# Latent attention and mLSTM on one core: the last sigmoid ahead of gate rows and weights, key rounding on VectorE, score products ahead of the last division

## The chip, the core and the metric

The kernel runs on one core of a Trainium2 chip. The metric is the device time of one execution in microseconds. The core has a matmul engine (TensorE, PE in the profile, with its weight loads as PEld), a vector engine (VectorE, DVE), an activation engine (ScalarE, ACT), GpSimd (POOL) and SyncE (SP), which issues the transfers. Each engine works through its own queue in order; semaphores order the engines among each other.

## The reference, cut to what matters

One step of a trunk of two layers over 640 tokens (128 context, 512 latent), model width 1024. Every layer is SwiGLU, mixer, SwiGLU. The mixer of layer 0 holds the change; it adds a latent attention with 8 heads to an mLSTM with 4 heads run in both directions over chunks of 128 tokens:

```python
q_a, kv_a, k_rope, mq, mk, mv, mo, mg = jnp.split(h @ w_in, EVEN_SPLIT_IDX, axis=-1)
ckv = rmsnorm(kv_a, g_kva)
q = (rmsnorm(q_a, g_qa) @ w_qb)                       # 8 heads of 64 + 32 (rope)
kv = keys_ckv @ w_kvb                                 # 8 heads of 64 (keys) + 64 (values)
k = concatenate([kv[..., :64], keys_kr (same for all heads)])
attn = softmax(q k^T / sqrt(96)) v
...                                                   # mLSTM, per head and direction, per chunk
a = einsum('bhtd,bhsd->bhts', qc, kc) * exp(dmat - mt)
hm = (h_forward + h_backward), rms-normalised, * g_mout
m_out = sigmoid(mo) * hm
y = concatenate([attn, m_out], -1) @ w_out
```

## The kernel before

Activations lie feature-major (features on partitions, 640 tokens on the free axis). Nearly all large products keep float32 precision with three passes: a weight tile is rounded by ACT to `w_hi` (L411), DVE subtracts to get `w_lo` (L417), and PE multiplies hi*hi, hi*lo and lo*hi. The same split is made for the operands of the attention scores: `k_top`/`k_rest` and `q_top`/`q_rest`. PSUM has 8 banks of 512 float32 columns; the code numbers them.

The mixer of layer 0 runs once, between some 540 and 900 us. It has three stages, in this order on every engine.

Input projection (`pe_even_in`, `act_even_in`, `dve_even_in`). Eight rounds of two weight chunks. The last two groups (`pe_token_major`) put token-major results into PSUM: `mv` into banks 0 to 4, then `mo` into banks 5, 6, 0, 1, 2, one bank per chunk of 128 tokens. ACT empties them with `fill(which, c)`: a copy into `v_m`, a sigmoid into `mo` (L804), each adding one to `l_vfill`. Between these ACT and DVE work on the small "rows" of the gates; `act_rows_columns` (L1233 to L1239) reads bank 7, takes exponentials into `floors` and raises `r_columns`. In the last round (b == 7) ACT's order is: round a weight chunk, four sigmoids, round the next weight chunk (the first one of the output projection), `act_rows_columns`, the fifth sigmoid, and then an activation table load (L1867). Before it starts the attention, PE waits for all ten `l_vfill` and for `r_columns`.

Latent attention (`pe_mla`, `act_mla`, `dve_mla`). The order of the work is a list, `MLA_PLAN`, built once by `mla_plan()`; each engine walks the same list and does its part of each entry. "swap", "turned", "keys", "queries" and "values" build q, k and v from the latent tensors (L552, L526, L535 on PE; copies on ACT, rope on DVE). For each head: "stage", "stage2" and "stage3" are ACT copies that round the raw query into `q_top` (L643, L644), the raw key into `k_top` (L646) and the rope rest into `q_rest` (L649); "rest" is DVE's two subtractions (L700, L702); nine "unit" entries are score products whose maxima DVE reduces (L573, L708) to a per-query shift; "shift" spreads the maxima (L577, L579), ACT writes them into `q_top` (L652). Seven "scores" entries (L593 to L595) make the scores of 128 keys by all queries, ACT takes the exponential (L658) and "attend" multiplies with the values (L603, L610). The units of head h+1 are interleaved with the scores x = 2, 3, 4 of head h; they wait for `e_hi`, which ACT raises at the end of `k_top`. ACT's entries for head h+1 stand behind scores 0 ("stage"), 1 ("stage2") and 3 ("stage3") of head h. "divisor" (ACT: Ln, Exp, L666, L668) and "divide" (DVE, L723, raising `e_scaled`) normalise a head, "high"/"low" (L671, L727) split the result of a pair of heads into `hx_hi`/`hx_lo`; "low" raises `o_done`.

mLSTM (`pe_mlstm`, `act_mlstm`, `dve_mlstm`). PE first waits for all four `o_done`, then makes the raw score products of keys and queries in six groups `KQ_GROUPS` (L1326; group (two, e) holds one or two chunks and one row half) and transposes the keys (L1316, banks 5 to 7); ACT scales the products into `kq` (L1400). DVE, after its own `o_done` wait, multiplies `mo` by the gain (L1444, five instructions) and then scales the transposed keys into `ktok` (L1447, L1449). With `kq` and `ktok` in place the chunk loop over `ML_PLAN` begins (L1305 on PE).

After it follow the output projection of the mixer and the other sub-layers, whose first transfers and roundings are triggered by counts (`w_used`), not by time.

## Time and profile before

| | us |
|---|---|
| median of 3 runs | 2782.93 |
| lowest and highest | 2778.52, 2784.07 |
| profiled execution, its own time | 2783.91 |
| its span in the trace | 2782.0 |
| PE busy, share of the span | 95% |
| DVE busy, share of the span | 54% |
| ACT busy, share of the span | 38% |
| mean granted clock of PE | 0.974 |

1.9 us of the profiled execution lie outside the span. The page counts PE as busy 95% of the time, but its slices between 600 and 900 us are the ones below nine tenths; the time of a stage is read there from the timeline of each engine, with the idle time before an instruction in brackets and the instruction that ended it. PEclk is the share of full clock granted to PE: 1.00 is 2.4 GHz and 0.50 is 1.2 GHz.

### The profile page before, as it was taken

How to read it: one execution, taken by the hardware profiler on the slowest of the kernel's cores; microseconds unless marked ns; L12 is line 12 of the kernel's file. 1: busy time of each engine (PE TensorE's matmuls, PEld its weight loads, DVE VectorE, ACT ScalarE, POOL GpSimd, SP SyncE). 2: the span in 40 equal slices, each digit the busy share in tenths (PEclk: the TensorE clock that was granted, in tenths of full speed). 3: DMA queues.
4: the chain of work that ended last, by engine and by line, in shares of the span. 5: the costliest groups of instructions: out<-in, count | busy, mean ns of one | idle time of the engine just before them, and what ended most of it. 6: DMA issues, size and time to landing. Idle time of an engine off the chain costs nothing.

```text
span 2782.0 us, 41236 instructions
## 1 busy us (share of the span) xinstructions
PE 2637.4 (95%) x16851; PEld 2498.3 (90%) x16871; DVE 1490.8 (54%) x2403; ACT 1053.1 (38%) x1599; POOL 3.7 (0%) x5
## 2 busy tenths in 40 slices
PE   6999999998887899999999999999989989999998
PEld 6999999885456889999999999999978889999998
DVE  6888434633446377753367775346565436322334
ACT  4333334444553453223345222334433345222333
POOL 0000000000000000000000000000000000000000
PEclk7999999999988999999999999999989999999999
DMA  6666244320000246533446553344210024322344
GB/s 239 208 203 207 77 134 147 133 71 24 1 0 24 61 148 203 187 114 103 146 140 196 191 187 98 110 148 140 89 45 1 1 61 119 102 74 75 107 149 139
DMA packets 87770, 320.18 MB, mean 115 GB/s; under 512 B 12486, under 2 KB 16598, under 8 KB 87126
## 3 DMA queue, kind: packets, MB, share of 16 engines
q1 hardware_dynamic: 87638, 318.37, 35.4%
q8 instruction: 88, 1.44, 0.2%
q14 instruction: 44, 0.36, 0.0%
HBM read 312.44 MB, written 3.23 MB: 113 GB/s over the span
## 4 chain that ended last, share of the span: by engine, by line
PE 85%; DVE 8%; ACT 4%; issue 2%; DMA 2%; SPq 1%; another core or an unknown queue 0%; DVEq 0%; ACTq 0%
PE ps L2179 42%; PE ps L2208 29%; PE ps L990 2%; PE ps L746 2%; DVE w_lo L417 1%; PE ps L603 1%; ACT w_hi L411 1%; DMA w_raw<-in_ffn_gu 1%; PE ps L552 1%; PE ps L2242 1%; PE ps L976 1%; DVE xsq L1967 1%; PE ps L979 1%; PE ps L978 1%; DVE hx_lo L1976 1%
## 5 line engine op out<-in xcount | busy, mean ns | idle before, releaser
L417 DVE TENSOR_TENSOR w_lo<-w_raw,w_hi 128x1024 fp32r<-128x1024 f32 (+1 forms) x384 | 521.0, 1358 | 901.5 <-ACT w_hi L411 898.7
L411 ACT CAST w_hi<-w_raw 128x1024 fp32r<-128x1024 f32 (+1 forms) x384 | 443.7, 1156 | 1212.5 <-PE ps L2179 715.1
L2179 PE MATMUL ps<-hx_hi,w_hi 128*128 128x320 f32 x2688 | 614.3, 309 | 11.8 <-DVE hx_lo L1526 5.7
L2179 PE MATMUL ps<-hx_lo,w_hi 128*128 128x320 f32 x2688 | 613.3, 309 | 0.0
L2179 PE MATMUL ps<-hx_hi,w_lo 128*128 128x320 f32 x2688 | 613.1, 309 | 0.0
L2179 PEld LDWEIGHTS ps<-hx_hi,w_hi 128*128 128x128 f32 x2688 | 451.4, 188 | 13.1 <-issue 7.6
L2179 PEld LDWEIGHTS ps<-hx_hi,w_lo 128*128 128x128 f32 x2688 | 451.8, 188 | 0.0
L2179 PEld LDWEIGHTS ps<-hx_lo,w_hi 128*128 128x128 f32 x2688 | 451.7, 188 | 0.0
L2208 PE MATMUL ps<-hh_hi,w_hi 128*128 128x320 f32 x1408 | 435.4, 309 | 3.0 <-DVE hh_lo L2071 3.0
L2208 PE MATMUL ps<-hh_hi,w_lo 128*128 128x320 f32 x1408 | 433.2, 308 | 0.0
L2208 PE MATMUL ps<-hh_lo,w_hi 128*128 128x320 f32 x1408 | 433.2, 308 | 0.0
L2208 PEld LDWEIGHTS ps<-hh_hi,w_hi 128*128 128x128 f32 x1408 | 263.9, 187 | 4.7 <-issue 3.9
L2208 PEld LDWEIGHTS ps<-hh_lo,w_hi 128*128 128x128 f32 x1408 | 263.9, 187 | 0.6
L2208 PEld LDWEIGHTS ps<-hh_hi,w_lo 128*128 128x128 f32 x1408 | 263.9, 187 | 0.0
L2208 PE MATMUL ps<-hx_hi,w_hi 128*128 128x320 f32 x672 | 222.0, 330 | 29.5 <-DVE hx_lo L1976 21.1
L2208 PE MATMUL ps<-hx_lo,w_hi 128*128 128x320 f32 x672 | 213.8, 318 | 0.0
L2208 PE MATMUL ps<-hx_hi,w_lo 128*128 128x320 f32 x672 | 213.8, 318 | 0.0
L2208 PEld LDWEIGHTS ps<-hx_hi,w_hi 128*128 128x128 f32 x672 | 131.0, 195 | 45.5 <-issue 21.3
L2208 PEld LDWEIGHTS ps<-hx_lo,w_hi 128*128 128x128 f32 x672 | 132.3, 197 | 0.5
L2208 PEld LDWEIGHTS ps<-hx_hi,w_lo 128*128 128x128 f32 x672 | 132.1, 197 | 0.0
L1904 DVE SCALAR_TENSOR_TENSOR ada_junk<-ring_a,cond_b 128x1024 f32<-128x1024 f32 x96 | 117.1, 1220 | 3.7 <-DVE ring_a L1904 0.5
L1904 DVE SCALAR_TENSOR_TENSOR ring_a<-ring_a,cond_b 128x1024 f32<-128x1024 f32 x96 | 117.1, 1220 | 0.0
(298 smaller groups left out, 2634.3 us busy)
## 6 DMA issues: line engine op xcount, KB each, us to landing
w_raw<-in_ffn_gu SPq DMA_DIRECT2D x212, 512.0 KB, 3.6
w_raw<-in_ffn_dn SPq DMA_DIRECT2D x128, 704.0 KB, 4.1
ring_a<-in_ada_w SPq DMA_DIRECT2D x96, 512.0 KB, 4.6
ada_top<-in_ada_w SPq DMA_DIRECT2D x32, 512.0 KB, 4.6
w_raw<-in_even_in SPq DMA_DIRECT2D x16, 512.0 KB, 3.6
w_raw<-in_odd_in SPq DMA_DIRECT2D x12, 512.0 KB, 4.7
first_a<-in_ada_w SPq DMA_DIRECT2D x8, 512.0 KB, 12.2
w_raw<-in_even_out SPq DMA_DIRECT2D x8, 512.0 KB, 3.7
```

What stands on the lines that cost most here:

```text
L411: nc.scalar.copy(w_hi[:, slot, 0:tiles * P], w_raw[:, slot, 0:tiles * P]).then_inc(hi_done, 1)
L417: nc.vector.tensor_tensor(w_lo[:, slot, 0:tiles * P], w_raw[:, slot, 0:tiles * P], w_hi[:, slot, 0:tiles * P], ALU.subtract).then_inc(lo_d ...
L552: ins = nc.tensor.matmul(ps[:, bank + n, 0:b - a], w_qb[:, k, tile * P:(tile + 1) * P], pa[:, k, a:b], start=(k == 0), stop=(k == 1))
L603: nc.tensor.matmul(ps[:, 6 + two, :], value_ones(x, h), prob_e[:, b % 3, :], start=(x == 0), stop=(x == 5)).then_inc(e_pv, 1)
L746: last = nc.tensor.matmul(ps[:, tok_bank(which, c), :], a[:, 2 * i + k, c * P:(c + 1) * P], w[:, q, cols], start=i == 0 and k == 0 and a i ...
L976: nc.tensor.matmul(out, ones_r[:], diag_o[:, g["g"] % 4].rearrange("p i q -> p (i q)"), start=True, stop=False)
L978: nc.tensor.matmul(by_head, k_hi[:, h, kcol:kcol + P], queries, start=False, stop=False)
L979: ins = nc.tensor.matmul(by_head, k_lo[:, h, kcol:kcol + P], queries, start=False, stop=side is None)
L990: ins = nc.tensor.matmul(ps[:, 6 + g["g"] % 2, i * (HEAD + 1):(i + 1) * (HEAD + 1)], prob_o[:, b % 4, i * P:(i + 1) * P], v_aug[:, g["bloc ...
L1904: ins = nc.vector.scalar_tensor_tensor(out=product, in0=tile, scalar=1.0, in1=cond_b[:, ci, :], op0=ALU.mult, op1=ALU.mult, accum_out=mods ...
L2179: last = nc.tensor.matmul(ps[:, out_bank + h, 0:TH], w, a[:, k, h * TH:(h + 1) * TH], start=(start and w is wh and a is hi), stop=(stop an ...
L2208: last = nc.tensor.matmul(ps[:, bank, 0:TH], w, a[:, k0 + t, half(h)], start=first and t == 0 and w is wh and a is hi, stop=last_chunk and ...
```

## The change

It does four things.

1. In the last round of the input projection ACT takes the fifth sigmoid first, then `act_rows_columns`, then the rounding of the next weight chunk. PE's wait for all sigmoids and for `r_columns` ahead of the attention is split: "swap" (now in banks 3 and 4) starts with the five `v_m` copies done, "turned" (banks 6 and 7) waits for two sigmoids and `r_columns`, "queries" (banks 0 and 1) for all sigmoids.
2. "stage2", the rounding of the key into `k_top`, is done by DVE with a semaphore of its own, `e_khi`; `e_hi` is raised at the end of ACT's query copies. "stage2" and "stage" stand together behind scores 0.
3. In the mLSTM, PE no longer waits for `o_done`. Groups (0,0), (0,1), (1,1), (2,0) of the score products follow the last attend at once; group (1,0), in bank 1, waits for the eighth `e_scaled`, and the transposes and group (2,1) follow it.
4. ACT scales the products into `kq` ahead of its wait for `o_done` and for the stored outputs.

```diff
--- before.py
+++ after.py
@@ -70,8 +70,8 @@
             if before:
                 plan.append(("attend",) + before)
             before = (h, x)
-            if h + 1 < MLA_HEADS and x in (0, 1, 3):
-                plan.append(({0: "stage", 1: "stage2", 3: "stage3"}[x], h + 1, 0))
+            if h + 1 < MLA_HEADS and x in (0, 3):
+                plan += [("stage2", h + 1, 0), ("stage", h + 1, 0)] if x == 0 else [("stage3", h + 1, 0)]
             if h and x in (2, 3):
                 plan.append(({2: "divisor", 3: "divide"}[x], h - 1, 0))
             if h + 1 < MLA_HEADS and x == (2 if h % 2 == 0 else 5):
@@ -332,7 +332,7 @@
         e_built, e_raw, e_vfill = sem("e_built"), sem("e_raw"), sem("e_vfill")
         e_rope_t, e_rope, e_rope_hi, e_rope_lo = sem("e_rope_t"), sem("e_rope"), sem("e_rope_hi"), sem("e_rope_lo")
         kr_ready, rows_clear, gates_moved = sem("kr_ready"), sem("rows_clear"), sem("gates_moved")
-        e_hi, e_rows, e_lo = sem("e_hi"), sem("e_rows"), sem("e_lo")
+        e_hi, e_khi, e_rows, e_lo = sem("e_hi"), sem("e_khi"), sem("e_rows"), sem("e_lo")
         e_unit, e_max, e_diag, e_shift, e_neg = sem("e_unit"), sem("e_max"), sem("e_diag"), sem("e_shift"), sem("e_neg")
         e_st, e_p, e_pv, e_inv, e_scaled = sem("e_st"), sem("e_p"), sem("e_pv"), sem("e_inv"), sem("e_scaled")
         odd_out, odd_turned, odd_rope = sem("odd_out"), [sem("odd_turned0"), sem("odd_turned1")], sem("odd_rope")
@@ -488,7 +488,7 @@
 
             if kind == "values":
                 return (2, 3, 4, 5, 0, 1, 6)[i]
-            return {("keys", 0): 4, ("turned", 0): 6}.get((kind, i), 0)
+            return {("swap", 0): 3, ("keys", 0): 4, ("turned", 0): 6}.get((kind, i), 0)
 
         def value_pairs(x):
 
@@ -541,11 +541,15 @@
                         pe.wait_ge(e_raw, 2 * i + 1)
                     else:
                         pe.wait_ge(e_rope_t, 1)
+                        pe.wait_ge(l_vfill, 2 * CHUNKS)
                 elif i:
                     if kind == "swap":
                         pe.wait_ge(e_raw, 5)
                     else:
                         pe.wait_ge(e_rope_t, 2)
+                elif kind == "turned":
+                    pe.wait_ge(l_vfill, CHUNKS + 2)
+                    pe.wait_ge(r_columns, 1)
                 tile = {"queries": i, "turned": 4 + 2 * i, "swap": 5 + 2 * i}[kind]
                 for n, (a, b) in enumerate(((CTX, T), (0, CTX))):
                     for k in range(2):
@@ -563,6 +567,7 @@
                     u, bank = 9 * h + x, 2 + (9 * h + x) % 2
                     if x == 0:
                         pe.wait_ge(e_hi, h + 1)
+                        pe.wait_ge(e_khi, h + 1)
                         if h == 0:
                             pe.wait_ge(e_vfill, 2)
                         else:
@@ -641,9 +646,7 @@
                     if h >= 2:
                         act.wait_ge(e_st, 7 * (h - 1))
                     nc.scalar.copy(q_top[0:64, two, :], raw_q[0:64, h % 2, :])
-                    nc.scalar.copy(q_top[64:96, two, :], rope_hi[stack_rows(h), :].bitcast(F32))
-                elif kind == "stage2":
-                    nc.scalar.copy(k_top[0:64, two, :], raw_k[0:64, h % 2, :]).then_inc(e_hi, 1)
+                    nc.scalar.copy(q_top[64:96, two, :], rope_hi[stack_rows(h), :].bitcast(F32)).then_inc(e_hi, 1)
                 elif kind == "stage3":
                     act.wait_ge(e_rope_lo, h // 4 + 1)
                     nc.scalar.copy(q_rest[64:96, two, :], rope_lo[stack_rows(h), :].bitcast(F32)).then_inc(e_rows, 1)
@@ -680,7 +683,12 @@
 
             for kind, h, x in MLA_PLAN:
                 two = h % 2 if h is not None else 0
-                if kind == "swap":
+                if kind == "stage2":
+                    dve.wait_ge(e_raw, 2 * (h // 2) + 1)
+                    if h >= 2:
+                        dve.wait_ge(e_st, 7 * (h - 1))
+                    nc.vector.tensor_copy(k_top[0:64, two, :], raw_k[0:64, h % 2, :]).then_inc(e_khi, 1)
+                elif kind == "swap":
                     dve.wait_ge(e_built, MLA_BUILT[kind, x])
                     nc.vector.tensor_tensor(rope_t[:], ps[:, build_bank(kind, x), :], rope_e[:, 1, :],
                                             ALU.mult).then_inc(e_rope_t, 1)
@@ -696,6 +704,7 @@
                     nc.vector.tensor_tensor(rope_lo[:, LAT:T], flat(bank, LAT, T), rope_hi[:, LAT:T].bitcast(F32),
                                             ALU.subtract).then_inc(e_rope_lo, 1)
                 elif kind == "rest":
+                    dve.wait_ge(e_khi, h + 1)
                     dve.wait_ge(e_hi, h + 1)
                     nc.vector.tensor_tensor(k_rest[0:64, two, :], raw_k[0:64, h % 2, :], k_top[0:64, two, :].bitcast(F32),
                                             ALU.subtract)
@@ -779,8 +788,7 @@
             pe_token_major(pe, chunk, 1, 2)
             pe_rows_columns(pe)
             pe_token_major(pe, chunk, 1, 3)
-            pe.wait_ge(l_vfill, 2 * CHUNKS)
-            pe.wait_ge(r_columns, 1)
+            pe.wait_ge(l_vfill, CHUNKS)
             pe.wait_ge(mix_loaded, 16 * 7)
             pe.wait_ge(lora_ready, 3)
             pe.wait_ge(attn_const, 6)
@@ -823,13 +831,14 @@
                     link(act, act_chain, nc.scalar.activation(halves(lora[:, 4, :]), bank_pair(3), ACT.Ln,
                                                               bias=eps_col[:, 0:1], scale=1.0 / P))
                     nc.scalar.activation(lora[:, 3:5, :], lora[:, 3:5, :], ACT.Exp, scale=-0.5).then_inc(lora_rstd, 1)
+                if b == 7:
+                    fill(1, CHUNKS - 1)
+                    act_rows_columns(act)
                 split_hi(act, 2 * b + chunk + 3, 1, 8)
                 if b < 4:
                     evacuate(2 * b + 1)
-                elif b == 7:
-                    act_rows_columns(act)
-                if b in (5, 7):
-                    fill(b // 7, CHUNKS - 1)
+                elif b == 5:
+                    fill(0, CHUNKS - 1)
                 if b == 3:
                     act.wait_ge(in_loaded, CONSTS)
                     zero, one = (ident[96:P, c:c + 1].unsqueeze(1) for c in (0, 96))
@@ -1188,7 +1197,7 @@
 
             return (j, 0) if u == 0 else (u - 1, j + 1)
 
-        KQ_GROUPS = [(two, e) for two in range(3) for e in range(2)]
+        KQ_GROUPS = [(0, 0), (0, 1), (1, 1), (2, 0), (1, 0), (2, 1)]
 
         def kq_chunks(two):
 
@@ -1308,7 +1317,6 @@
                     ins = nc.tensor.matmul(ps[:, d, :], ident_b[:], causal_b[:, d].rearrange("p i q -> p (i q)"),
                                            start=False, stop=True)
                 return ins
-            pe.wait_ge(o_done, MLA_OUT)
             def turned_keys():
                 for c in range(CHUNKS):
                     for j in range(2):
@@ -1316,6 +1324,8 @@
                         ins = nc.tensor.transpose(ps[:, 5 + c // 2, a:a + P], mqk[:, 2 + j, c * P:(c + 1) * P], ident[:])
                 ins.then_inc(l_turned, 1)
             for two, e in KQ_GROUPS:
+                if (two, e) == (1, 0):
+                    pe.wait_ge(e_scaled, MLA_HEADS)
                 if (two, e) == (2, 1):
                     turned_keys()
                     pe.wait_ge(l_kq, len(KQ_GROUPS) - 1)
@@ -1392,14 +1402,14 @@
 
         def act_mlstm(act):
 
-            act.wait_ge(o_done, MLA_OUT)
-            act.wait_ge(out_stored, 48)
             for i, (two, e) in enumerate(KQ_GROUPS):
                 act.wait_ge(l_turned, i + 1 + (i == len(KQ_GROUPS) - 1))
                 cs, a = kq_chunks(two), kq_start(two, e)
                 nc.scalar.activation(kq[:, e::2, cs[0]:cs[-1] + 1, :].rearrange("p h c q -> p c h q"),
                                      ps[:, kq_bank(two, e), a:a + 256 * len(cs)].rearrange("p (c h q) -> p c h q", h=2, q=P),
                                      ACT.Copy, scale=M_DK ** -0.5).then_inc(l_kq, 1)
+            act.wait_ge(o_done, MLA_OUT)
+            act.wait_ge(out_stored, 48)
             for kind, u in ML_PLAN:
                 two = u % 2
                 if kind == "decays":
```

## Rows read from the trace of the kernel before

**Rows 1.** Timeline of ACT, 654 to 660: start, duration, instruction [idle before, releaser]

```profile
654.37 1.04 ACT L411 CAST w_hi<-w_raw 128x1024 fp32r<-128x1024 f32 x1 [1.15 <-PE ps L746]
...
657.00 0.21 ACT L1239 ACTIVATE floors<-ps 128x16 f32<-128x16 f32 x1
...
658.52 0.60 ACT L804 ACTIVATE mo<-ps 128x512 f32<-128x512 f32 x1
```

**Rows 2.** Timeline of PE, start of the attention, same columns

```profile
659.17 7.51 PE L552 MATMUL ps<-pa,w_qb 128*128 128x512 f32 x16 [5.19 <-ACT mo L804]
...
668.02 2.33 PE L552 MATMUL ps<-pa,w_qb 128*128 128x512 f32 x8
```

**Rows 3.** Windows: length, busy PE, PEld, DVE, ACT, POOL, PEclk, DMA, GB/s

```profile
659.00:660.00 1.00, 0.83 (x1) 0.50 (x2) 0.00 (x0) 0.98 (x2) 0.00 (x0) 0.50 0.00 0
...
788.00:789.50 1.50, 1.50 (x6) 1.11 (x5) 0.69 (x1) 0.20 (x1) 0.00 (x0) 0.50 0.00 0
...
849.50:851.00 1.50, 1.50 (x8) 1.50 (x8) 1.47 (x4) 0.78 (x2) 0.00 (x0) 0.50 0.98 391
```

**Rows 4.** Timelines of DVE, ACT and PE ahead of the first maxima

```profile
655.45 1.23 DVE L417 TENSOR_TENSOR w_lo<-w_raw,w_hi 128x1024 fp32r<-128x1024 f32 x1 [6.51 <-ACT w_hi L411]
...
677.24 2.75 DVE L708 TENSOR_REDUCE e_mx<-ps 128x1 f32<-128x512 f32 x5
...
668.17 0.62 ACT L629 CAST rope_hi<-rope_raw 128x512 fp32r<-128x512 f32 x1 [7.76 <-DVE rope_raw L691]
...
674.53 0.94 ACT L646 CAST k_top<-raw_k 64x896 fp32r<-64x896 f32 x1
...
675.80 1.03 PE L573 MATMUL ps<-k_top,q_top 96*128 96x512 f32 x2
```

**Rows 5.** Waits, 683 to 826: who waited for whom, us in total, times, longest

```profile
PE ps L573 <- ACT k_top L646: 11.4, 7, 1.9
```

**Rows 6.** Timelines: ACT and PE at head 2's first unit, DVE at head 5's

```profile
707.61 0.72 ACT L644 CAST q_top<-rope_hi 32x640 fp32r<-32x640 f32 x1
...
708.97 0.94 ACT L646 CAST k_top<-raw_k 64x896 fp32r<-64x896 f32 x1
...
709.96 0.50 PE L573 MATMUL ps<-k_top,q_top 96*128 96x512 f32 x1 [1.92 <-ACT k_top L646]
...
767.57 0.69 DVE L708 TENSOR_REDUCE e_mx<-ps 128x1 f32<-128x512 f32 x1 [5.32 <-PE ps L573]
```

**Rows 7.** Groups of instructions, 683 to 826: busy us, mean ns, idle before

```profile
L700 DVE TENSOR_TENSOR k_rest<-raw_k,k_top 64x896 fp32r<-64x896 f32 x7 | 7.5, 1075 | 0.0
```

**Rows 8.** Timeline of PE: the first units of heads 1 and 4

```profile
689.97 0.50 PE L573 MATMUL ps<-k_top,q_top 96*128 96x512 f32 x1 [0.72 <-ACT k_top L646]
...
752.41 0.50 PE L573 MATMUL ps<-k_top,q_top 96*128 96x512 f32 x1 [1.29 <-ACT k_top L646]
```

**Rows 9.** Timeline of PE: shift of head 4, first unit and shift of head 6

```profile
760.57 0.50 PE L577 MATMUL ps<-diag_e,ones_r 128*128 128x512 f32 x1
...
787.55 0.50 PE L573 MATMUL ps<-k_top,q_top 96*128 96x512 f32 x1 [1.79 <-ACT k_top L646]
...
797.34 0.51 PE L577 MATMUL ps<-diag_e,ones_r 128*128 128x512 f32 x1
```

**Rows 10.** Timelines of DVE, ACT and PE, from the last division to the chunk loop

```profile
827.37 0.90 DVE L723 TENSOR_TENSOR o_raw<-ps,e_rec 64x512 f32<-64x512 f32 x2 [5.44 <-ACT e_rec L668]
...
829.92 3.10 DVE L1444 TENSOR_TENSOR mo<-mo,w_raw 128x512 f32<-128x512 f32 x5
...
836.80 1.23 DVE L1447 TENSOR_SCALAR ktok<-ps 128x1024 f32<-128x1024 f32 x1 [3.78 <-PE ps L1316]
...
828.31 0.72 ACT L671 CAST hx_hi<-o_raw 128x640 fp32r<-128x640 f32 x1 [0.97 <-DVE o_raw L723]
...
829.94 5.30 PE L1326 MATMUL ps<-mqk 64*128 64x128 f32 x36 [4.16 <-DVE hx_lo L727]
...
838.50 1.26 PE L1305 MATMUL ps<-gstack,pick 128*128 128x128 f32 x8 [1.10 <-DVE ktok L1449]
```

## The prediction

> **What bounds the kernel now.** I read the page first, then the timelines of PE, ACT and DVE from 636 to 862 us, the list of waits between 683 and 826, and the granted clock in short windows. The page's part 1 has PE busy nearly throughout, so away from the mixer of layer 0 a reordering of the other engines has nothing to win, and the change touches nothing there. In this mixer PE stands idle in three places, and the timeline names the releaser of each. Ahead of the attention it is idle 5.19 us, and the fifth sigmoid ends it [rows 2]. In the attention it waits for the rounding of `k_top` seven times, 11.4 us in total [rows 5]. After the last head it waits 4.16 us for `hx_lo` [rows 10]. That is 20.7 us. A second cost goes with it: behind such a gap the granted clock can be at its lower level, 1.2 GHz (0.50), for some microseconds [rows 3]. Everything behind the mixer waits on counts of finished work, so what is gained here arrives at the end one to one.
>
> **Part 1: the end of the input projection.** PE's last product ends at 653.98 (659.17 less 5.19) [rows 2]. ACT reacts at 654.37 with the weight rounding of 1.04, then come the gate rows, then the fifth sigmoid until 659.12 [rows 1]. With the change PE begins "swap" at once: its banks 3 and 4 held `v_m`, emptied long before. "Swap" and "turned" are 16 records and took 7.51 us from a low clock [rows 2, 3]; 8 such records at the full clock take about 2.2 (2.33 with the drain of the last) [rows 2]. With no gap the clock stays up, so "swap" ends at about 656.1.
> "Turned" must wait for `r_columns`. This was raised at 657.21, 1.80 us after the rounding had ended at 655.41 [rows 1]. Now a sigmoid of 0.60 stands in the place of that rounding: 654.37 + 0.60 + 1.80 = 656.8. "Turned" runs from 656.85 to about 659.0 instead of ending at 666.6: 7.6 us earlier. A table load (back to the sigmoid's set) falls away too, off this path.
> The weight rounding moves behind the gate rows, to 656.7 to 657.8, and DVE's `w_lo` of 1.23 [rows 4] follows it, to 659.0. It stands in DVE's queue ahead of the rope of "swap", finished by PE at 656.1. Who waits for that: "queries" on PE, which stands behind "keys" and is needed near 660.5, while the rope is ready at 659.7, so no cost; and the rope of "turned", which comes out about 0.45 late. ACT's chain therefore starts with `rope_hi` at 661.05 instead of 668.17 [rows 4], 7.1 earlier. The weight chunk itself, and SP's next load into its slot, are used only after the mLSTM, 200 us later; no cost.
> In the first head ACT's `k_top` ended at 675.47 and DVE's first maximum started at 677.24, 1.77 after it, because DVE's "rest" lies between [rows 4]. With `k_top` on DVE (in its idle time before 667), "rest" waits for ACT's `q_top` alone, which ended when `k_top` began, at 674.51. So "rest" starts at 674.51 - 7.1 = 667.4 and the first maximum at 669.2. PE's first unit comes at 675.80 [rows 4] less 7.6, 668.2, and is done by then. DVE's maxima set the time here, and they are 677.24 - 669.2 = 8.0 us earlier. **Part 1 with the first head: 8.0 us.**
>
> **Part 2: heads 1 to 7.** At head 2 ACT does `q_top` until 708.33, an exponential of 0.60, then `k_top` until 709.91, and PE starts the first unit at 709.96 after 1.92 idle [rows 6]. With `k_top` off ACT, the unit is released at 708.38, 1.58 earlier. DVE is idle there: the shortest gap before a head's first maximum is 5.32 [rows 6], so its copy is hidden, and I cost it at nothing. No row of before has a DVE copy of this form. Its time lies between that of ACT, 0.94 [rows 6], or somewhat less, and that of DVE's subtraction over as many elements, 1.08 [rows 7]; I take 1.0, and if the cover were gone the seven would cost 7 us. The copy waits for the scores of head h-1; behind that wait DVE's queue holds only this head's maxima, which need the copy anyway.
> PE's idle is 0.72 and 1.29 before heads 1 and 4 [rows 8], which leaves 11.4 - 2.0 = 9.4 for the other five [rows 5], 1.88 each. The gains are 0.72 + 1.29 + 5 x 1.57 = 9.9. What is late next is ACT's `q_top`, by 0.3. The second wait per first unit may cost 0.04 each (an estimate: 0.05 lies between a releaser's end and PE's start [rows 6]), 0.3 in all. **9.6 us.**
> The clock: from first unit to shift head 4 took 760.57 - 752.41 = 8.16, head 6 with the same work 797.34 - 787.55 = 9.79 [rows 8, 9], with 0.50 granted at its start [rows 3]. A fall costs 1.6 there. Heads 5 and 7 have falls too; DVE's "rest" covers part of them, and I take 0.7 each, between 0 and 1.6. All three follow a gap of nearly 2 us that shrinks to 0.3: **3.0 us**, bounds 0 and 4.8.
> [...]
>
> **Part 3: into the mLSTM.** PE ends the attention at 825.78 (829.94 less 4.16). Four groups of score products follow at once, and group (1,0) finds its division done at 828.27 [rows 10]. Even at the pace of before, products and transposes take what they took from 829.94 to 836.80, 6.86, and end at 832.7. ACT starts on `kq` after `hx_hi`, at 829.03 [rows 10], and needs at most 0.60 each (the sigmoid of the same shape [rows 1]): five are done by 832.1, in time for group (2,1). DVE's work on `mo` ends at 829.92 + 3.10 = 833.02. DVE was then idle 3.78 us for the transposes; now `ktok` starts at 833.05 instead of 836.80 and the chunk loop at 834.75 instead of 838.50 [rows 10]: **3.75 us**. What is late next is the work on `mo`, that is `o_done` itself. ACT's last `kq` stays hidden behind `ktok`. The moved wait for stored outputs costs nothing: they are issued at the end of the input projection.
> The Trainium skill (TensorE: Matmul & The Clock Gate, Part 4) says that transposes do not count as PE activity. By it the clock could fall in the wait for `ktok`, behind the ten transposes; the first 8 spread records, 1.26 [rows 10], would then take up to twice that, and this part would be 2.5. No row here shows it.
>
> **The sum.** 8.0 + 9.6 + 3.0 + 3.75 = 24.4 us. The profiled execution took 2783.9 (span 2782.0 and 1.9 around it), 1.0 above the median. 2783.9 - 24.4 = 2759.5, or 2758.5 against the median. I say 2759.
>
> **The rivals.**
> First, the clock gives nothing. Low spells come elsewhere when the gaps are gone: the 3.0 in the heads stay, and "swap" and "turned" (or what follows them) lose again what the full clock gave them, 7.51 - 4.4 = 3.1. Gain 18.3, time 2765.6. For it: the mLSTM, with its short bursts, has such a spell while PE is busy [rows 3]. Against: the spells at 659 and 788 both follow idle time.
> Second, the heads do not move, because what is left of ACT's chain or DVE's maxima hold them: 8.0 + 3.75 = 11.8, time 2772. Against: PE's wait names `k_top` in seven heads of seven [rows 5].
> Third, slower: DVE's in-order queue. Were the wait for the old scores reached late, or the copy held behind "rest" and maxima, each first unit would come later than ACT delivered it. Seven heads at d each outweigh parts 1 and 3 from d = 11.8 / 7 = 1.7 us on, that is if the copy of head 2 ends after 711.6. With d = 3 the time is 2783.9 - 11.8 + 21 = 2793. Against: 5.32 us of idle DVE at the tightest place [rows 6].
> Fourth, part 1 does not do what it says: "turned" waits on `r_columns` long enough for the clock to fall, and only 3 of the 8.0 us come. Time 2764.5.
>
> **How the numbers follow.** Forecast 0.62 (its own range 2753 to 2764); first and fourth rival 0.26; second 0.08; third 0.02; the rest, near no change, 0.02. A measurement tells 0.2% from no change, 5.6 us, so under 2777.4 is faster: faster 0.95, same 0.03, slower 0.02. The low end, 2752, takes in the lowest run of before (4.4 below the median) and one more low spell gone. The high end takes in the first and fourth rival and half of the way to the second: 2769.
>
> **What would show it.** Right: the first L552 near 654 with no sigmoid as releaser, `rope_hi` near 661, PEclk 1.00 there; at most 0.4 us idle before each head's first unit, ended by `q_top`; head 6 at 8.2 us from unit to shift; the first L1326 with no idle before it, and `ktok` directly behind the work on `mo`. Wrong: `k_top` from DVE later than `q_top`, 1 us of idle or more before the units with another name in the brackets, or a PEclk of 0.50 where it was 1.00.

## The result and the profile after

| | before | after |
|---|---|---|
| median, us | 2781.38 (4 runs) | 2757.95 (4 runs) |
| lowest and highest | 2778.52, 2784.07 | 2757.47, 2759.45 |
| profiled execution, its own time | 2783.91 | 2759.45 |
| its span | 2782.0 | 2757.6 |

The ratio of the times is 0.9923, with a 95% interval from 0.9909 to 0.9938: 21.4 us, and 17 to 25 by the interval. The two profiled executions are 24.46 us apart; the forecast for them was 24.4. That of before lies 2.5 us above its median and that of after 1.5 above its own. The page of after:

```profile
span 2757.6 us, 41258 instructions
...
PE 2629.5 (95%) x16851; PEld 2495.4 (90%) x16871; DVE 1495.8 (54%) x2411; ACT 1043.6 (38%) x1590; POOL 3.7 (0%) x5
```

The shares of the page are what they were. The change is seen only in timelines, stage by stage. First the end of the input projection, in the timelines of ACT, PE and DVE of after (start, duration, instruction, and in brackets the idle time before it and the releaser):

```profile
654.11 0.60 ACT L812 ACTIVATE mo<-ps 128x512 f32<-128x512 f32 x1 [0.80 <-PE ps L755]
...
654.80 1.28 ACT L1245 ACT_TABLE_LOAD   x1
...
656.35 1.07 ACT L411 CAST w_hi<-w_raw 128x1024 fp32r<-128x1024 f32 x1
...
660.63 0.62 ACT L634 CAST rope_hi<-rope_raw 128x512 fp32r<-128x512 f32 x1 [1.92 <-DVE rope_raw L699]
...
653.91 2.32 PE L556 MATMUL ps<-pa,w_qb 128*128 128x512 f32 x8
656.63 2.40 PE L556 MATMUL ps<-pa,w_qb 128*128 128x512 f32 x8 [0.40 <-ACT floors L1248]
...
668.14 1.03 PE L578 MATMUL ps<-k_top,q_top 96*128 96x512 f32 x2
...
674.99 0.80 PE L582 MATMUL ps<-diag_e,ones_r 128*128 128x512 f32 x1 [1.57 <-DVE diag_e L723]
...
663.15 0.62 DVE L690 CAST k_top<-raw_k 64x896 fp32r<-64x896 f32 x1 [0.82 <-ACT raw_k L631]
...
668.98 2.77 DVE L717 TENSOR_REDUCE e_mx<-ps 128x1 f32<-128x512 f32 x5
```

Of the idle time before the first L556, 5.19 us in [rows 2], nothing is left for "swap", and 0.40 for "turned". `rope_hi` comes 7.54 us earlier than in [rows 4], the first maximum 8.26 us, and the shift of head 0 (the spread of its maxima) 8.06 us (683.05 before).

Then the heads. Timeline of PE in after, the first units of heads 2 and 6, the queries ahead of head 4 and the shift of head 6:

```profile
699.96 0.50 PE L578 MATMUL ps<-k_top,q_top 96*128 96x512 f32 x1 [0.35 <-ACT q_top L649]
...
731.87 2.43 PE L556 MATMUL ps<-pa,w_qb 128*128 128x512 f32 x8 [1.71 <-DVE rope_lo L704]
...
769.10 0.50 PE L578 MATMUL ps<-k_top,q_top 96*128 96x512 f32 x1 [0.21 <-ACT q_top L649]
...
777.25 0.50 PE L582 MATMUL ps<-diag_e,ones_r 128*128 128x512 f32 x1
```

The list of waits of after, in the attention (us in total, times, longest):

```profile
PE ps L578 <- ACT q_top L649: 1.5, 5, 0.4
```

Windows of after (length, busy PE, PEld, DVE, ACT, POOL, then PEclk, DMA share and GB/s):

```profile
672.00:676.00 4.00, 2.03 (x5) 1.08 (x4) 3.02 (x7) 0.07 (x1) 0.00 (x0) 0.50 0.00 0
676.00:680.00 4.00, 3.33 (x7) 2.45 (x8) 0.00 (x0) 2.25 (x4) 0.00 (x0) 0.50 0.00 0
...
690.00:790.00 100.00, 90.94 (x327) 51.89 (x325) 55.71 (x104) 60.36 (x101) 0.00 (x0) 1.00 0.00 1
812.00:816.00 4.00, 2.74 (x9) 2.17 (x10) 0.87 (x3) 1.40 (x6) 0.00 (x0) 0.50 0.30 70
```

The row of [rows 5], 11.4 us in seven waits for `k_top`, has become 1.5 us in five waits for `q_top`. The windows show the other half of it: 1.00 granted over a hundred microseconds of heads, where before had 0.50 at 788 [rows 3]. But they also show a low spell (a stretch at 0.50) at 672 to 682.5, before and behind head 0's shift, and one at 812, at the start of the mLSTM.

Last, the way into the mLSTM, in the timelines of ACT, DVE and PE of after:

```profile
807.07 2.32 ACT L1408 ACTIVATE kq<-ps 128x512 f32<-128x512 f32 x5
...
808.06 3.10 DVE L1454 TENSOR_TENSOR mo<-mo,w_raw 128x512 f32<-128x512 f32 x5
811.18 1.23 DVE L1457 TENSOR_SCALAR ktok<-ps 128x1024 f32<-128x1024 f32 x1
...
803.85 3.77 PE L1336 MATMUL ps<-mqk 64*128 64x128 f32 x36
807.55 1.31 PE L1324 MATMUL ps<-ident,mqk 128*128 128x128 f32 x10
809.45 0.71 PE L1336 MATMUL ps<-mqk 64*128 64x128 f32 x4 [0.59 <-ACT kq L1408]
812.89 2.29 PE L1314 MATMUL ps<-gstack,pick 128*128 128x128 f32 x8 [2.73 <-DVE ktok L1459]
...
892.02 0.56 PE L2189 MATMUL ps<-hx_hi,w_hi 128*128 128x320 f32 x2 [1.59 <-DVE w_lo L417]
```

`ktok` follows the work on `mo` with no idle, where DVE had waited 3.78 us [rows 10]. The chunk loop starts 25.61 us earlier than before (812.89 against 838.50), and its first eight products take 2.29 us where they took 1.26 [rows 10]. The row at 892.02 belongs to the output projection behind the mLSTM. The timeline of PE in before has it at 916.47:

```profile
916.47 0.56 PE L2179 MATMUL ps<-hx_hi,w_hi 128*128 128x320 f32 x2 [1.60 <-DVE w_lo L417]
```

The lead there is 24.45, and it stays so to the end: from that row on both kernels take the same time, 1865.6 and 1865.5 us of the span.

### The profile page after: what moved, and what is told of

Same layout as the page of the kernel before. It is cut to its first block, busy times and chain, and to the rows that moved or that the text cites. A ratio compares the mean times of both kernels' runs of the same rounds, so it can differ in the third digit from the quotient of the medians.

```text
span 2757.6 us, 41258 instructions
## 1 busy us (share of the span) xinstructions
PE 2629.5 (95%) x16851; PEld 2495.4 (90%) x16871; DVE 1495.8 (54%) x2411; ACT 1043.6 (38%) x1590; POOL 3.7 (0%) x5
## 4 chain that ended last, share of the span: by engine, by line
PE 84%; DVE 7%; ACT 4%; DMA 2%; issue 2%; SPq 1%; another core or an unknown queue 0%; DVEq 0%; ACTq 0%
PE ps L2189 42%; PE ps L2218 29%; PE ps L999 2%; PE ps L755 2%; DVE w_lo L417 1%; PE ps L608 1%; ACT w_hi L411 1%; DMA w_raw<-in_ffn_gu 1%; PE ps L2252 1%; PE ps L985 1%; PE ps L556 1%; PE ps L988 1%; PE ps L987 1%; PE ps L578 0%; DMA w_raw<-in_odd_in 0%
```

## The experiments

The theory: the three parts act at their own places and add up, and a part of the gain in the heads is the clock's. Its rivals: the clock gives nothing; the copy on DVE is near its limit; the parts cover each other. Each ratio is against runs of the kernel before on the same chip. Timelines and windows are of one execution of each kernel.

### Each part alone

**e1, part 1 alone.**

```diff
-            pe.wait_ge(l_vfill, 2 * CHUNKS)
-            pe.wait_ge(r_columns, 1)
+            pe.wait_ge(l_vfill, CHUNKS)
...
+                if b == 7:
+                    fill(1, CHUNKS - 1)
+                    act_rows_columns(act)
                 split_hi(act, 2 * b + chunk + 3, 1, 8)
```

> The first part alone (fifth sigmoid first, swap in banks 3 and 4, split waits); heads and mLSTM as before. Theory (gains by idle time removed, clock kept up through swap and turned, one to one to the end): first maximum of head 0 near 669.0 instead of 677.2, and 8.0 us at the end, time about 2776 against a profiled before of 2783.9. Rival (the clock gives nothing): swap and turned fast, but a low spell later; gain 5. The unknown between them is which heads have a low spell once all is shifted by 8 us: each costs 0.7 to 1.7.

Measured: median 2772.33, ratio 0.9971 (0.9962 to 0.9981), that is 8.1 us, 5 to 11 by the interval. "Turned" in the timeline of PE:

```profile
656.30 1.10 PE L556 MATMUL ps<-pa,w_qb 128*128 128x512 f32 x2 [0.40 <-ACT floors L1243]
```

The heads' wait in the list of waits (us in total, times, longest):

```profile
PE ps L577 <- ACT k_top L650: 10.6, 6, 1.9
```

The start is that of after, and the heads wait for `k_top` as in before (the first of the seven waits lies ahead of the stretch of this list, 683 to 826). Head 0's shift comes at 675.51, 7.54 us earlier than before: in head 0 the rounding of the key is still ACT's here.

**e2, part 2 alone.**

```diff
+                if kind == "stage2":
+                    dve.wait_ge(e_raw, 2 * (h // 2) + 1)
+                    if h >= 2:
+                        dve.wait_ge(e_st, 7 * (h - 1))
+                    nc.vector.tensor_copy(k_top[0:64, two, :], raw_k[0:64, h % 2, :]).then_inc(e_khi, 1)
```

> The second part alone (key rounding on DVE, e_hi at the end of the query copies). Theory: idle before the first units shrinks from 11.4 to about 1.5 us, worth 9.6, and the low spells inside heads 5, 6 and 7 go with the gaps, worth 3.0 and perhaps the one at 743 (1.7) as well; head 6 takes 8.2 us from first unit to shift. Gain 12.6 to 14.3, time 2769.6 to 2771.3. Rival (clock gives nothing): gain 9.6, time 2774.3. Rival (heads held elsewhere): under 3.

Measured: median 2767.63, ratio 0.9958 (0.9943 to 0.9972), 11.7 us, 8 to 16 by the interval. Timeline of PE, first unit and shift of head 6:

```profile
775.01 0.50 PE L574 MATMUL ps<-k_top,q_top 96*128 96x512 f32 x1 [0.22 <-ACT q_top L645]
...
783.16 0.50 PE L578 MATMUL ps<-diag_e,ones_r 128*128 128x512 f32 x1
```

A window over the heads, with PEclk third from the end:

```profile
690.00:810.00 120.00, 109.68 (x393) 62.95 (x392) 62.35 (x117) 70.28 (x118) 0.00 (x0) 1.00 0.00 1
```

Head 6 takes 8.15 us from unit to shift, against 9.79 in [rows 9], and no window of the heads is below full clock. The spells in them go with part 2 alone. The median gained less than the 12.6 to 14.3 us expected, and its interval takes in that range as well as the rival's 9.6.

**e3, part 3 alone.**

```diff
-        KQ_GROUPS = [(two, e) for two in range(3) for e in range(2)]
+        KQ_GROUPS = [(0, 0), (0, 1), (1, 1), (2, 0), (1, 0), (2, 1)]
...
-            pe.wait_ge(o_done, MLA_OUT)
...
+                if (two, e) == (1, 0):
+                    pe.wait_ge(e_scaled, MLA_HEADS)
```

> The third part alone (score products of the mLSTM behind the last attend, key scaling copies ahead of the wait for o_done). Theory: ktok starts directly behind the work on mo, 3.75 us earlier relative to the end of the attention, of which about 1 is lost when the clock falls in the wait for ktok, so that the spread products run at 1.2 GHz; gain 2.8 to 3.8, time 2780 to 2781. If the three parts add up, e1, e2 and e3 give 8.0 + 13.5 + 3 = 24.5; a sum off by over 2 would mean that a part's gain hangs on another's.

Measured: median 2777.41 of 10 runs against 2779.3 of 20, ratio 0.9997 (0.9987 to 1.0007): 0.8 us, and 3.6 at most by the interval. Timeline of PE:

```profile
822.98 3.77 PE L1327 MATMUL ps<-mqk 64*128 64x128 f32 x36
...
832.02 1.64 PE L1305 MATMUL ps<-gstack,pick 128*128 128x128 f32 x5 [2.73 <-DVE ktok L1450]
```

From the end of the attention to the chunk loop it takes 9.0 us (822.98 to 832.02), before took 12.72 (825.78 to 838.50), after 9.0. So the 3.7 us are gained at their place. From there to the first product of the output projection it takes 59.60 us, and 58.42 in the profiled execution of before: 1.2 go back. What is left, some 2.5, a timing of this kernel hardly tells from nothing.

That 2.5 hangs on the one execution of before. Kernels e1 and e2 above and e5 below have its mLSTM too. From the end of the attention to the output projection before took 71.14 us, and e1, e2 and e5 took 72.06, 72.32 and 72.00; after took 68.62, e3 68.64 and e11, which is after once more, 68.51. By these part 3 is worth 2.5 to 3.8 us.

The three ratios fall short of 1 by 0.0029, 0.0042 and 0.0003, together 0.0074, and the whole change by 0.0077. The parts add up as far as such intervals can tell, which is some 6 us (a rough estimate from the four intervals); that none covers another is seen better in the timelines, each part acting at its own place.

### The cover of the copy

**e4, the copy three times.** After, with two superfluous copies ahead of each one that counts:

```diff
+                    for _ in range(2):
+                        link(dve, dve_chain, nc.vector.tensor_copy(k_top[0:64, two, :], raw_k[0:64, h % 2, :]))
```

> The changed kernel, with DVE's rounding of the key done three times in a row (each waits for the one before) for every head. One copy took 0.62 us, so each head's k_top is ready about 1.4 us later. Theory (the copy is hidden, q_top on ACT releases the unit): no change, idle before the first units of heads 2, 3 and 7 stays 0.35 and is still ended by q_top; time within 0.5 us of the changed kernel (2759.5 profiled). Rival (DVE's queue sets the heads): 7 x 1.4 = 10 us slower, 2769.

Measured: median 2758.27, ratio 0.992 (0.9904 to 0.9937), as after. Timelines of DVE and PE at head 2:

```profile
694.26 1.27 DVE L691 CAST k_top<-raw_k 64x896 fp32r<-64x896 f32 x2 [3.00 <-PE ps L600]
695.57 0.62 DVE L692 CAST k_top<-raw_k 64x896 fp32r<-64x896 f32 x1
...
698.84 0.50 PE L578 MATMUL ps<-k_top,q_top 96*128 96x512 f32 x1 [0.35 <-ACT q_top L649]
```

The third copy ends at 696.2, the unit starts 2.6 us later, and it is still `q_top` that releases it, after the same 0.35 us. The slower rival, DVE's in-order queue, was far from deciding there, and the median shows nothing of it either.

### What the clock gives

**e5, the gaps of before filled.** Before, with five superfluous score products (into the bank that the next unit overwrites) ahead of the first units of heads 2 to 7, where PE waits for `k_top` anyway:

```diff
+                    if x == 0 and h:
+                        pe.wait_ge(e_neg, h)
+                        pe.wait_ge(e_max, u - 1)
+                        for n in range(5 if h > 1 else 0):
+                            nc.tensor.matmul(ps[:, bank, 0:512], q_top[0:MLA_QK, 1 - two, 0:P],
+                                             k_top[0:MLA_QK, 1 - two, 0:512], start=True, stop=True)
```

> The kernel before, with five superfluous score products (96x128 by 512, 0.235 us each at the full clock, some 1.2 us together) ahead of PE's wait for the first unit of heads 2 to 7, written into the bank that the unit then overwrites. The first unit is still released by k_top, so no wait ends earlier. Theory (the gap costs twice: once as idle time and once by the lower clock behind it): the low spells behind the first units of heads 5, 6 and 7 and the one at 743 do not appear, the time falls by 2 to 5 us below the kernel before and scatters less than its 2772.6 to 2783.9. Rival (the clock gives nothing, the gain of the second part is idle time alone): low spells at the same or other places, time unchanged.

Measured: median 2779.21, ratio 0.9992 (0.9983 to 1.0002). Windows over the heads, first of this kernel:

```profile
694.00:821.00 127.00, 115.44 (x417) 68.06 (x418) 57.24 (x109) 75.65 (x123) 0.00 (x0) 1.00 0.00 0
```

then of the kernel before:

```profile
694.00:825.00 131.00, 114.32 (x387) 65.59 (x387) 57.47 (x109) 75.06 (x123) 0.00 (x0) 0.95 0.00 0
```

With the gaps filled the clock stays at 1.00 and the attention takes 162.4 us, where the profiled execution of before took 166.6. But e3, whose attention is that of before, took 163.8: how many of the gaps are followed by a fall differs from one execution to the next. The traces of all kernels tell it best between the shift of head 1 and that of head 7 (us, from the timelines of PE):

| | head 1's shift | head 7's shift | between | low spells |
|---|---|---|---|---|
| before | 702.82 | 813.80 | 110.98 | 4 |
| e1, same heads | 695.27 | 805.77 | 110.50 | 4 |
| e3, same heads | 702.22 | 811.09 | 108.87 | 3 |
| e5, gaps filled | 702.58 | 809.43 | 106.85 | 0 |
| after | 694.39 | 791.96 | 97.57 | 0 |

The other eight kernels with part 2 (e2, e4 and e6 to e11) took 97.51 to 97.58, and none has a spell there. So the spells do follow from the gaps: they cost 4.1, 3.7 and 2.0 us in the three executions, and the gaps themselves 9.3.

The medians of before and e5 are only 1.6 us apart, under the 2 to 5 expected, and the interval takes in no change. A part may be that e5's low spell in heads 0 and 1 is longer: it ends at 692.6, that of before at 689.0, and from the shift of head 0 to that of head 1 e5 took 1.24 us more. The scatter did change: ten runs within 2.9 us, while those of before range over 10.7 (13 runs on that chip), and those of e1 and e3, which keep the gaps, over 11.9 and 9.6. The gaps are not its only cause: e7 and e10, which have none in these heads, range over 11.2 and 9.3.

**e9, "swap" waits too.** After, with the waits of before ahead of "swap" (ACT's new order stays):

```diff
-            pe.wait_ge(l_vfill, CHUNKS)
+            pe.wait_ge(l_vfill, 2 * CHUNKS)
+            pe.wait_ge(r_columns, 1)
```

> The changed kernel with PE's waits for all sigmoids and r_columns back ahead of swap; ACT's new order and the banks stay. PE is then idle from 654.0 to 656.6. Theory (the fourth rival is a matter of the gap's length; before, the clock fell 4.6 us after PE had stopped): the gap of 2.6 us is too short for a fall, swap and turned stay at the full clock and end at 661.1 instead of 658.9, 2.2 us slower at the first maximum and at the end, 2760. Rival (any idle wait costs the clock): turned ends near 664, 5 us slower, 2763.

Measured: median 2760.25, ratio 0.9926 (0.9908 to 0.9944). After itself, run beside it as **e11** with no edit, gave 2757.7, ratio 0.9919 (0.9901 to 0.9937).

> The changed kernel as it is, to have it on the same chip beside e9 and e10. Expected 2758, and 0.992 of the kernel before; heads without low spells again, low spells at 671 to 683 and from 812 on.

Timeline of PE in e9:

```profile
655.70 6.25 PE L556 MATMUL ps<-pa,w_qb 128*128 128x512 f32 x16 [2.52 <-issue]
```

and a window of it:

```profile
656.00:660.00 4.00, 4.00 (x9) 1.90 (x8) 1.33 (x2) 1.81 (x2) 0.00 (x0) 0.57 0.02 4
```

(`issue` stands where the profile shows no releaser; by the code the wait is for the fifth sigmoid and `r_columns`.) A gap of 2.52 us was enough for a fall here: the sixteen products took 6.25 us, against 2.32 and 2.40 in after. That I had not expected of so short a gap. Head 0's shift comes at 677.73, in e11 at 674.46: 3.3 us for a gap of 2.5 us, which replaces one of 0.4. The medians are 2.5 apart, with intervals that overlap. In part 1, then, some 60 to 70% is ACT's order, and the rest that "swap" waits for nothing.

### The start of the mLSTM

**e6, 18 superfluous transposes** and **e7, 11 superfluous products** in the wait for `ktok`, into a free bank, both on after:

```diff
+            for n in range(18):
+                nc.tensor.transpose(ps[:, 3, P * (n % 4):P * (n % 4) + P], mqk[:, 2 + n % 2, 0:P], ident[:])
```

```diff
+            for n in range(11):
+                nc.tensor.matmul(ps[:, 3, P * (n % 4):P * (n % 4) + P], mqk[:, 2 + n % 2, 0:P], mqk[:, n % 2, 0:P],
+                                 start=True, stop=True)
```

> The changed kernel, with 18 superfluous transposes of 128x128 (0.13 us each, 2.4 us together) in PE's 2.73 us gap between the last score products of the mLSTM and the spread products. Theory A (transposes do not count as PE activity): the clock still falls near 812 and the first 8 spread products still take 2.3 us; time as the changed kernel, 2758. Theory B (only idle time lets it fall): they take 1.26 and the fall comes later or not; up to 1 us faster.

> The same gap filled with 11 superfluous products of 128x128 (22 records of 0.11 us, 2.4 us together). Both theories: the clock stays up at 812, the first 8 spread products take 1.26 us and the chunk loop gains about 1 us there, of which the later low spells in the loop may take some back. If e6 and e7 look alike, what fills the gap does not matter; if only e7 keeps the clock, transposes do not count.

Measured: medians 2754.9 and 2756.73, ratios 0.9904 (0.9888 to 0.9921) and 0.9904 (0.988 to 0.9928). Timeline of PE in e6:

```profile
809.58 2.19 PE L1340 MATMUL ps<-ident,mqk 128*128 128x128 f32 x18
812.38 0.63 PE L1314 MATMUL ps<-gstack,pick 128*128 128x128 f32 x4 [0.61 <-DVE ktok L1461]
```

windows of e6:

```profile
811.00:815.00 4.00, 2.25 (x17) 1.72 (x15) 1.54 (x3) 1.59 (x7) 0.11 (x1) 0.99 0.29 66
815.00:819.00 4.00, 1.57 (x7) 1.57 (x8) 1.83 (x4) 0.59 (x3) 0.00 (x0) 0.50 0.00 0
```

and one of e7:

```profile
811.00:815.00 4.00, 3.58 (x29) 3.10 (x28) 2.00 (x3) 0.78 (x4) 0.91 (x1) 1.00 0.24 66
```

In both the clock stays up over the first products of the chunk loop; four take 0.63 us again, and for that what fills the wait, transposes or products, makes no difference. Then it falls all the same, at 815 in e6, in the next wait, and near 819 in e7. From the first product of the loop to L1363 of after (L1353 before) it takes 5.05 us in both, in after 5.76, and to the output projection 57.36 and 56.96, in after 59.58 and in e11 59.47. The medians lie 3 and 1 us under that of after, no more than the intervals leave open.

**e8, the work on `mo` ahead of the last division.** After, with DVE's five products of `mo` by the gain in the 5.44 us in which it waits for the last `e_rec`:

```diff
+                    if h == MLA_HEADS - 1:
+                        dve.wait_ge(l_vfill, 2 * CHUNKS)
+                        for c in range(CHUNKS):
+                            by = mo[:, c, :].rearrange("p (n v) -> p n v", n=2)
+                            ins = nc.vector.tensor_tensor(by, by, gm, ALU.mult)
+                        ins.then_inc(o_gated, 1)
```

> The changed kernel, with DVE's multiplication of mo by the gain (5 instructions, 3.10 us) moved ahead of the last division, where DVE is idle 5.44 us. Theory (in the changed kernel ktok is late because of this work alone): ktok starts behind the transposes, near 808.9 instead of 811.18, the spread products near 810.6 instead of 812.89, released by ktok or kq; 2.2 us faster, and the shorter gap keeps the clock up, another 0 to 1; time 2755 to 2756. Rival (the transposes or ACT's kq are just as late): under 0.5 us.

Measured: median 2755.43, ratio 0.9905 (0.9889 to 0.9922). Timelines of DVE and PE:

```profile
799.10 3.08 DVE L732 TENSOR_TENSOR mo<-mo,w_raw 128x512 f32<-128x512 f32 x5
804.62 0.90 DVE L738 TENSOR_TENSOR o_raw<-ps,e_rec 64x512 f32<-64x512 f32 x2 [2.44 <-ACT e_rec L671]
...
808.11 1.23 DVE L1458 TENSOR_SCALAR ktok<-ps 128x1024 f32<-128x1024 f32 x1 [0.97 <-PE ps L1330]
...
809.82 0.63 PE L1320 MATMUL ps<-gstack,pick 128*128 128x128 f32 x4 [0.54 <-ACT kq L1414]
```

The five products fit into the wait, and `ktok` now waits for PE's transposes. From the end of the attention to the loop it takes 6.9 us instead of 9.0, the 2.2 expected; the medians differ by 2.3 from e11, inside the intervals. The wait of 2.73 us that the change left behind is to be had.

The clock did not stay up, though. PE is idle only 0.59 and 0.54 us ahead of the loop here, and yet the clock falls at 810.9, as this window shows, and stays low until 824.6:

```profile
811.00:815.00 4.00, 0.70 (x3) 0.19 (x2) 2.15 (x4) 2.03 (x8) 0.00 (x0) 0.50 0.25 66
```

So the long wait for `ktok` is not needed for a fall in this place. What e6 and e7 show is that with superfluous work in it the fall comes later.

**e10, both ends.** e8, and superfluous products in head 0's gaps, where DVE's maxima hold PE:

```diff
+                    for n in range(0 if h else 6 if x == 8 else int(x > 0)):
+                        nc.tensor.matmul(ps[:, 7, :], q_top[0:MLA_QK, 0, 0:P], k_top[0:MLA_QK, 0, 0:512],
+                                         start=True, stop=True)
...
+                    for n in range(0 if h else 3):
+                        nc.tensor.matmul(ps[:, 7, :], q_top[0:MLA_QK, 0, 0:P], k_top[0:MLA_QK, 0, 0:512],
+                                         start=True, stop=True)
```

> e8 (mo by the gain ahead of the last division) and superfluous score products of head 0 between the DVE-bound units (one behind each of units 1 to 7, six behind the last, three behind the spread of the maxima; into bank 7, free then). The changed kernel has its longest low spell there, 671 to 683. Theory: the clock stays up, the six score products behind the first shift take 0.235 instead of 0.43 each, head 1's first unit comes 1 to 2.5 us earlier; time 2 us below e8, 2753. Rival (PE cannot fit them without delaying the units, or the spell only moves): no faster than e8.

Measured: median 2748.14, ratio 0.9895 (0.9877 to 0.9914), the lowest median of all; 2753 was expected. Its window from the attention to the mLSTM:

```profile
653.00:810.00 157.00, 144.10 (x542) 84.10 (x540) 82.70 (x150) 93.83 (x165) 3.54 (x1) 1.00 0.00 1
```

No spell is left there, and the chunk loop starts at 808.04, 1.8 us before that of e8. But by the first product of the output projection that is lost again (868.86 against 868.52): the spells of the mLSTM are longer. And the five runs are in two groups, 2747.59 to 2748.14 and 2756.2 to 2756.84; the profiled one is of the slower group. So the low median is not explained by the window above. One run of e7 (2748.41) and the profiled one of e6 (2750.15) are as low. In the latter the part behind the mixer took 1859.0 us instead of 1865.6, with a mean granted clock of 0.981 over the span, against 0.976 in after. Its code is the same there. That the clock is the cause fits these numbers, but no run isolates it.

## Why the prediction was right, point by point

**Part 1 and the first head: forecast 8.0, seen 8.06 to head 0's shift, alone 8.1 by the medians (5 to 11) and 7.54 to head 0's shift.** Each station came where it was put, to 0.5 us: "swap" ended at 656.23 (656.1 forecast), "turned" began at 656.63 (656.85), `rope_hi` at 660.63 (661.05), the first unit at 668.14 (668.2), the first maximum at 668.98 (669.2). The clock stayed up over "swap" and "turned", the weight rounding behind the gate rows delayed nobody, and DVE's maxima set the time in head 0. The fourth rival, a long wait for `r_columns`, falls with the 0.40 us; e9 shows that its mechanism was near: in its profiled execution 2.5 us of waiting were followed by a fall there.

**Part 2, the waits: forecast 9.6, seen 9.9** (11.4 of [rows 5] less 1.5). `q_top` is what is late next, as said. The 0.04 for the second wait cannot be seen. The assumed copy time was wrong: 1.0 us, with 0.94 (or somewhat less) and 1.08 as its bounds, where the rows show 0.62. It cost nothing because the copy is hidden even three times over (e4).
The Trainium skill (VectorE: DVE Perf Modes, "The perf-mode tier table") gives copies of float32 within SBUF twice the rate of two-operand instructions. The trace agrees: 0.62 against 1.08 for the subtraction over as many elements [rows 7]. Weighed in the prediction, it would have moved the bound and not the sum.

**The clock in the heads: forecast 3.0, seen 2.5 at the places named and 1.7 elsewhere.** From first unit to shift, head 6 gave 1.64 (9.79 to 8.15), head 5 0.68 (13.53 to 12.85), head 7 0.19 (9.86 to 9.67). Not forecast was the spell at the queries ahead of head 4, which took 4.12 us before and 2.43 after, though the gap ahead of them, 1.71 us with `rope_lo` as releaser, is the same in both. In the timeline of PE before:

```profile
743.42 4.12 PE L552 MATMUL ps<-pa,w_qb 128*128 128x512 f32 x8 [1.71 <-DVE rope_lo L696]
```

Against it stand 0.35 us in head 1. Waits and clock together: 9.9 + 2.5 + 1.7 - 0.35 = 13.75, and the attention behind head 0's shift is shorter by 13.8 (21.86 less 8.06), against 12.6 forecast.
This term is right for the execution that was profiled, and others with the same gaps would have given 3.7 and 2.0 in heads 2 to 7 (e1, e3). The medians say less: e5 took the spells away and moved that of before by 1.6 us, with an interval that takes in no change. By the medians the rival "the clock gives nothing" is not refuted for this term alone; it is refuted by the traces. Which gaps are followed by a fall could not be told ahead: in before heads 2 and 3, with gaps of 1.92 and 1.93 us, had none, and head 7 with 1.93 had one.
The Trainium skill (TensorE: Matmul & The Clock Gate, "HAM oscillation") tells of a kernel that waited for a transfer in every step and whose clock fell anew in every step. The waits there are longer than the gaps here, so it sets no price for them; this case's trace shows falls behind shorter ones, 1.71 to 1.93 us.

**Part 3: forecast 3.75, seen 3.7 at its place and some 2.5 behind it.** The waits went as forecast: no idle before the score products, `ktok` directly behind the work on `mo`. The step that was mis-sized is that nothing would be given back: behind the wait of 2.73 us for `ktok` the granted clock is 0.50, and the eight products after it take 2.29 us instead of 1.26. Up to the output projection the mLSTM takes 59.58 instead of 58.42 for the profiled pair. In e1, e2 and e5, whose mLSTM is that of before, it took 60.44, 59.11 and 60.37, so the 1.16 is in good part luck of the one execution of before.
The Trainium skill (TensorE: Matmul & The Clock Gate, "Part 4") had led to 2.5, which is about what was measured. Its reason isn't borne out here: e6 fills the same wait with transposes alone, and over the next products the clock stays up as with e7's products. Nor is the wait the whole cause, as e8 shows; what sets the moment of the fall stays open.

**The sum.** 8.06 + 13.8 + 3.75 - 1.16 = 24.45 for the profiled pair, against 24.4. That the total fits to 0.1 us is partly luck: 1.2 more in the heads and 1.2 less in the mLSTM cancel, and both hang on which spells the profiled execution of before had. The medians moved by 21.4 to 23.4 us (ratio and plain difference).

**The low spells.** The first rival said that they would come elsewhere. In part they did: the one in heads 0 and 1 grew from about 7 to 10.5 us (672 to 682.5), and another appeared at 812. The growth is not settled: in e11, the same kernel as after, that spell lasts about 7 us again (674 to 680.7). e10, which fills head 0's waits for DVE, has none. In the profiled pair head 1 gained 0.35 us less than its wait, and the mLSTM lost 1.2.

## What to carry to other kernels

On an engine that works in order, look at what stands ahead of the instruction that others wait for: moving one 0.60 us sigmoid ahead of a rounding and of the gate rows with their table load, with the wait behind it split, gave 8 us, and a copy moved to an engine idle for 5 us there gave 10. Make the sum of such waits from one trace: here each held to 0.3 us at its place. Put the clock's share in as a range, since it differs from one execution to the next (2.0 to 4.1 us in the same heads). A gain of 2 to 4 us in 2780 is seen in the trace at its place, but hardly in the medians: do the parts together, and read each from the timeline.

## What the runs showed of the hardware

- The gap of 1.71 us ahead of the queries of head 4 was followed by a low clock in before and by the full one in after. The same code with the same gaps of about 1.9 us is followed by a granted clock of 0.50 in some heads and not in others. Three executions with such gaps in heads 2 to 7 had 4, 4 and 3 low spells there (before, e1, e3), ten without them had none.
- A gap of 2.52 us behind steady products was followed by 0.57 over the next 4 us (e9), one of 2.73 between short products by 0.50 (after). In e8 gaps of 0.59 and 0.54 us near the same place were followed by 0.50 too, from 810.9 on.
- The granted clock stayed at 0.50 for 8 us (672 to 680 in after), over stretches in which PE was busy 2.03 and 3.33 us of 4.
- DVE rounds 64x896 float32 from SBUF to SBUF in 0.62 us, where ACT takes 0.94 [rows 4].
- Two groups of times, 8 us apart, in kernels that differ from after only by superfluous or moved work in the mixer (e10, one run of e7); what tells the groups apart is open.
